# Dense products in pairs on half of the array's rows, with weights in common pieces

## What is computed

```python
def first_block(x, ...):                       # 1 layer
    proj = rmsnorm(x, norm_mix) @ w_in         # q, kv, gates, GLA q k v, merge gates
    o_a = nsa_attention(...)                   # compressed + selected + window softmax
    o_b = gla_chunked(...)                     # gated linear attention
    merged = gate_a * (o_a @ w_up_nsa) + gate_b * (o_b @ w_up_gla)
    x = x + merged @ w_out
    h = rmsnorm(x, norm_ffn)
    x = x + (silu(h @ w_ffn_gate) * (h @ w_ffn_up)) @ w_ffn_down   # D_FF = 2816
    return rmsnorm(x, norm_final)

def second_block(x, ...):                      # 4 layers: mla0, swa, fox, mla1
    y = branch(x)      # h = x @ w_in; 16-head causal (mla, fox) or windowed (swa) softmax; (o * silu(gate)) @ w_out
    x = layernorm(DEEPNORM_ALPHA * x + y)
```

## Time and profile before

| | |
|---|---|
| median of 3 runs | 1986.87 us (1982.08 to 1987.17) |
| profiled execution | 1982.91 us, its span 1980.8 us |
| PE busy | 1854.9 us, 94% of the span, 10060 matmuls |
| PEld / DVE / ACT / POOL busy | 74% / 50% / 36% / 31% |
| mean granted TensorE clock | 0.976 of full |
| chain that ended last | PE 74%, DVE 18%, ACT 5% |

### The profile page before, as it was taken

How to read it: one execution, slowest core, us unless ns; L and a number is a source line. 1 busy time by engine, 2 the same in 40 slices (tenths; PEclk the granted TensorE clock), 3 DMA queues, 4 the chain that set the end, 5 groups by cost and what they waited for, 6 DMA issues and landing times.

```text
span 1980.8 us, 24915 instructions
## 1 busy us (share of the span) xinstructions
PE 1854.9 (94%) x10060; PEld 1469.7 (74%) x10060; DVE 996.3 (50%) x1964; ACT 717.4 (36%) x1533; POOL 621.6 (31%) x296
## 2 busy tenths in 40 slices
PE   6998799999999999999999989889999999999997
PEld 5777666788888888889666777767777777886665
DVE  4457687421410101144777456674655344576675
ACT  4342255323422222234444234442243233254450
POOL 3332111244344353434212223223423223331221
PEclk9998799999999999999999999989999999999998
DMA  4322110244233232334112222112422222321111
GB/s 158 88 75 56 53 33 22 61 120 138 84 98 107 85 106 85 96 88 93 36 43 77 64 86 65 53 54 64 117 64 75 64 64 71 94 50 44 47 56 61
DMA packets 215026, 148.44 MB, mean 75 GB/s; under 512 B 51952, under 2 KB 197120, under 8 KB 214912
## 3 DMA queue, kind: packets, MB, share of 16 engines
q1 hardware_dynamic: 210160, 135.40, 24.4%
q10 hardware_dynamic: 4752, 11.46, 1.7%
HBM read 144.74 MB, written 2.10 MB: 74 GB/s over the span
## 4 chain that ended last, share of the span: by engine, by line
PE 74%; DVE 18%; ACT 5%; issue 1%; DMA 1%; ACTq 0%; POOL 0%; SPq 0%; DVEq 0%
PE PS L386 19%; PE PS L387 19%; PE PS L388 19%; PE PS L474 6%; PE PS L528 5%; DVE P L1470 3%; PE PS L557 2%; ACT P L1024 2%; DVE X L1403 1%; DVE P L1881 1%; PE PS L687 1%; DVE X L1407 1%; DVE ST L1430 1%; DVE X L1421 1%; DVE sm L1867 1%
## 5 line engine op out<-in xcount | busy, mean ns | idle before, releaser
L1964 POOL TENSOR_TENSOR Wl<-Wr,Wh 128x1024 fp32r<-128x1024 f32 (+5 forms) x292 | 621.4, 2139 | 1321.7 <-ACT Wh L958 1321.7
L386 PE MATMUL PS<-XTl,Wh 128*128 128x512 f32 (+1 forms) x1096 | 416.2, 380 | 12.3 <-DVE XTl L1415 6.7
L387 PE MATMUL PS<-XTh,Wl 128*128 128x512 f32 (+1 forms) x1096 | 412.2, 376 | 0.0
L388 PE MATMUL PS<-XTh,Wh 128*128 128x512 f32 (+1 forms) x1096 | 411.6, 376 | 0.0
L958 ACT CAST Wh<-Wr 128x1024 fp32r<-128x1024 f32 (+5 forms) x292 | 267.6, 936 | 202.3 <-PE PS L388 179.6
L386 PEld LDWEIGHTS PS<-XTl,Wh 128*128 128x128 f32 x1096 | 209.5, 191 | 59.7 <-issue 12.8
L388 PEld LDWEIGHTS PS<-XTh,Wh 128*128 128x128 f32 x1096 | 209.4, 191 | 36.9
L387 PEld LDWEIGHTS PS<-XTh,Wl 128*128 128x128 f32 x1096 | 209.4, 191 | 35.3
L386 PE MATMUL PS<-Wl,XTh 128*128 128x512 f32 (+2 forms) x608 | 228.4, 376 | 3.7 <-DVE XTl L1415 3.7
L388 PE MATMUL PS<-Wh,XTh 128*128 128x512 f32 (+2 forms) x608 | 225.0, 370 | 0.0
L387 PE MATMUL PS<-Wh,XTl 128*128 128x512 f32 (+2 forms) x608 | 224.7, 370 | 0.0
(11 more groups left out here) (309 smaller groups left out, 2452.0 us busy)
## 6 DMA issues: line engine op xcount, KB each, us to landing
Wr<-in_w_in SPq DMA_DIRECT2D x38, 512.0 KB, 3.7
Wr<-in_fox_w_in SPq DMA_DIRECT2D x32, 512.0 KB, 3.9
Wr<-in_w_ffn_gate SPq DMA_DIRECT2D x22, 512.0 KB, 3.8
Wr<-in_w_ffn_up SPq DMA_DIRECT2D x22, 512.0 KB, 3.8
Wr<-in_w_ffn_down SPq DMA_DIRECT2D x22, 512.0 KB, 3.5
Wr<-in_swa_w_in SPq DMA_DIRECT2D x20, 512.0 KB, 3.7
Wr<-in_mla_w_in SPq DMA_DIRECT2D x16, 512.0 KB, 4.1
Wr<-in_mla_w_out SPq DMA_DIRECT2D x16, 512.0 KB, 3.5
```

The lines of the kernel that those rows point to most:

```text
L386: pe.matmul(o, l[0], r[1], start=start, stop=False)
L387: pe.matmul(o, l[1], r[0], start=False, stop=False)
L388: return pe.matmul(o, l[0], r[0], start=False, stop=stop)
L1964: raw.tensor_tensor(l[:, 0:m], r[:, 0:m], h[:, 0:m].bitcast(F), sub).then_inc(*weight_lo.next(i))
```

## The change

- `duo` issues two products together: for each of the three parts one matmul on 64 contraction rows for the one product and one on the other 64 rows for the other product, into different banks. `quad` does this for four products in two pairs, first all on one half of the rows, then swapped. A semaphore, `half_done`, holds a product's second half back until its first half is complete.
- `rows_part`, `outproj` and `first_N` go through it. `first_N` pairs tiles 0, 1 and 2 with each other (`THREE`), in six runs of 12 pairs, and does tile 3 in full rows behind its transposes. `outproj` completes both halves of a tile together: with a norm behind it the order is tile 0 first half, tile 1 first half, tile 0 second half, tile 1 second half, then tile 2, tile 3.
- `four_T` replaces `first_T` everywhere and `proj_T` in part: GLA q and k, the merge gate `gb`, `ua`/`ub`, all FFN gate and up products, the first four gates of mla, the first four products of swa and of fox. Its weights come as pieces of 2 feature blocks by 512 columns for the four products together.
- The groups of the FFN are 8, 8, 6. Single gates, queries and keys between attention steps stay `proj_T` in full rows, and `KX` (the compression) too.

```diff
+            def duo(one, two, h):
+                for n, (x, y) in enumerate(((0, 1), (1, 0), (0, 0))):
+                    ins = [pe.matmul(o, l[x][half(u + h)], r[y][half(u + h)], start=start and n == 0, stop=stop and n == 2)
+                           for u, (o, l, r, start, stop) in enumerate((one, two))]
+                return ins
+            def quad(blocks, first, last, flip, ready):
+                marks, ins = {}, {}
+                for g in range(2):
+                    for x in (0, 2):
+                        e.wait_ge(*([marks[x]] if g else ready(x) + ready(x + 1)))
+                        for n, products in enumerate(blocks):
+                            start, stop = first and g == n == 0, last and g == 1 and n == len(blocks) - 1
+                            ins[x], ins[x + 1] = duo(*[(*p, start, stop) for p in products[x:x + 2]], g ^ flip)
+                        if g == 0:
+                            ins[x + 1].then_inc(*half_done.next())
+                            marks[x] = half_done.now()
+                return ins
...
+                for tiles in THREE:          # THREE = ((0, 1), (2, 1), (2, 0), (1, 0), (1, 2), (0, 2))
+                    e.wait_ge(*[marks[t] for t in tiles if t in marks])
...
+                                e.wait_ge(weight_lo.at(i), *free(bs[t]), normed(before[s], t))
...
+                turn_tile(before[s], 3)
+                e.wait_ge(*free(bs[3]), normed(before[s], 3))
+                for i, a, r in blocks:
+                    ins = mm3(PS[bs[3]][:, 0:n], pair(XT, ALL, r, tile(3)), part(i, a, n), r == 0, r == kts - 1)
...
+                if norm:
+                    for i, h in ((0, 0), (1, 0), (0, 1), (1, 1)):
+                        tile_end(i, h)
+                    for i in (2, 3):
+                        tile_end(i, 0)
+                        if turned:
+                            turn_tile(s, i - 2)
+                        tile_end(i, 1)
+                    if turned:
+                        turn_tile(s, 2)
...
+            for g, n in enumerate((8, 8, 6)):
+                for f in range(f0, f0 + n, 2):
+                    cs = slice(128 * f, 128 * f + 256)
+                    four_T([((nm, f + x), XT, (reader, (nm, f + x))) for nm, reader in (("fg", by_act), ("fu", by_dve)) for x in range(2)],
+                           [(wg[:, :, cs], 0), (wu[:, :, cs], 256)], [normed("mix", 3)], None if f else "ffn")
```

More of the change, by code:

```diff
@@ L404, in proj_T, with four_T @@
                 give(b, *readers)
[L406 to L410, removed]
+            def four_T(products, srcs, ready, s=None):
+                bs = [take(p[0]) for p in products]
+                ws = split(srcs, 512)
+                kts = srcs[0][0].shape[1]
+                for h, c in enumerate(HALF_T if s else [ALL]):
                     if h:
@@ L412, in first_T @@
                         turn_tile(before[s], 3)
[L413 to L419, removed]
@@ L420, in first_T @@
-                for (_, b), (_, _, readers) in zip(ws, products):
-                    give(b, *readers)
+                    for n, (i, j, k) in enumerate(ws):
+                        e.wait_ge(weight_lo.at(i), *([normed(before[s], 2 * h + 1)] if s else ready))
+                        ins = quad([[(PS[b][:, c], part(i, a, 512, 128 * x, 128 * x + 128), pair(p[1], ALL, j + a, c))
+                                     for x, (b, p) in enumerate(zip(bs, products))] for a in range(k)],
+                                   j == 0, j + k == kts, n % 2, lambda x: free(bs[x]))
+                        if j + k < kts and c != HALF_T[0]:
+                            ins[3].then_inc(*weight_used.next())
+                            used[i] = weight_used.now()
@@ L423, in first_N @@
+                for x, p in enumerate(products):
+                    ins[x].then_inc(*done(psum_full, *p[0]))
+                    give(bs[x], *p[2:])
+                used[ws[-1][0]] = psum_full.now()
             def first_N(s, key, src, n, reader):
                 bs = [take((*key, t)) for t in range(NT)]
[L426 to L444, removed]
@@ L445, in first_N, with rows_part @@
                 for t in range(NT):
                     give(bs[t], (reader, (*key, t)))
[L448 to L460, removed]
+            def rows_part(key, bs, i, a1, k, kts, n, flip, lhs, ready):
+                e.wait_ge(weight_lo.at(i))
+                ins = quad([[(PS[b][:, 0:n], pair(lhs, ALL, a1 + a, tile(t)), part(i, a, n)) for t, b in enumerate(bs)] for a in range(k)],
+                           a1 == 0, a1 + k == kts, flip, lambda t: free(bs[t]) + ready(t))
+                if a1 + k == kts:
+                    for t in range(NT):
+                        ins[t].then_inc(*done(psum_full, *key, t))
+                    used[i] = psum_full.now()
+                else:
+                    ins[3].then_inc(*weight_used.next())
+                    used[i] = weight_used.now()
@@ L498, in outproj @@
-                    ins.then_inc(*weight_used.next())
+                    for g in range(2):
+                        for i in range(NT):
+                            if g:
+                                e.wait_ge(marks[i])
+                            ins = tile_part(w, a, i, (a + g) % 2, a == g == 0, False)
+                            if g == 0:
+                                ins[1].then_inc(*half_done.next())
+                                marks[i] = half_done.now()
+                    ins[1].then_inc(*weight_used.next())
```

156 lines of the change are left out of this document (94 added, 62 removed).

## The result

The changed kernel takes **2054.12 us** (2052.25 to 2055.67, 4 runs) beside 1986.09 of the kernel before on the same chip (1982.08 to 1987.17, 4 runs): ratio 1.0346, interval [1.0328, 1.0364]. It is slower by 68 us, outside the predicted range. The profiled execution has a span of 2050.2 us, against 1980.8.

A forecast was written before the change was run, and what follows sets the result against it. It took PE's matmul stream as the bound, with stretches where DVE releases PE. From 1982.9 us it took 69 and added 22, 6, 9, 6 and 1: 1958, carried to the median 1962; range 1922 to 2024.

The forecast's parts named there:

- What bounds the kernel: Whole kernel: mostly a matmul stream on PE, weight loads hidden; pairs could win only 0.013 to 0.020 us per matmul.
- Term 1: Dense product streams: a 512-column pair comes every 0.2145 us, as in float32 score rows; saving 69 us with narrower pairs.
- Rival 1: Matmul streams: pairs cost what full matmuls do, 0.227 to 0.234 us, so 2018 us, slower; chance 0.24.
- Term 2: Norms behind outproj: DVE ready 3.6 us later at four layer norms; 22 us, plus 6 at mix and ffn.
- Term 4: Start of outproj: TensorE waits for banks, about 1.1 us three times and 3 us at mix; 6 us.
- lost savings: Pitch savings not redeemed behind late norms: 5.6 us in four tails, 1 us each at swa and fox first products.
- Term 3: First product of the mla stages: waits for tile 2; costs 5.3 us at mla1, about 4 at mla0, sum 9.
- Term 5: Changes between full and half rows: 0.09 us each, net 1 us; half_done taken at nothing.

The follow-up runs named there:

- tile_by_tile: Changed kernel with tiles 0 and 1 finished one after the other in outproj's tail, not interleaved, still as half-row pairs: 2037.77 us.
- before_tail3: Kernel before with outproj's tail of three contraction blocks instead of four where a norm follows: 2005.83 us, ratio 1.0080.
- full_rows: Changed kernel, order kept, with every half-row pair of the dense products put back as full-row matmuls: 2036.16 us, ratio 1.0238.
- old_joints: Changed kernel with outproj, first_N, first products of ffn, swa and fox and the gates' order as before, pairs elsewhere kept: 1992.45 us, ratio 1.0028.
- full_outproj: Changed kernel with only outproj's matmuls on full rows, in the changed order: 2048.58 us.
- micro: Separate kernel, TensorE alone running streams of 192 matmuls, full rows, pairs or one half, several types and widths: reduced type at 512 columns 0.2267 us each.
- micro2: Second kernel of TensorE alone, varying stationary operand, stationary columns and moving columns: 0.2267 us in outproj's form, with pairs or without.

## Why the prediction was wrong

- **What bounds the kernel**: right. The stream is the bound, 0.013 us per matmul is all that pairs could have won, and loads are hidden.
- **Term 1, the step that failed**: "type is where they differ", said of the float32 score rows, from which the pitch of 0.2145 was taken. The pair pitch is 0.227 in the kernel and 0.2267 alone, so the term is 0 us instead of the 69 forecast. Rows of before could not settle it, but they could have weighed it: the leftover was seen in the reduced type on full rows and not in float32 on half rows; two things differed, and I gave the change to rows. Rival 1 named the other reading, and its threshold of 0.221 decided. The Trainium skill, "TensorEngine Tiling (Array Packing)", The Problem, which promises nothing for a contraction of 128 rows, agrees with the runs.
- **Term 2, norms late**: right in mechanism and nearly in size. 3.6 us were forecast; the table has 4.0 to 4.6 per layer norm, and tile_by_tile and before_tail3 show that DVE's first tile sets it. With term 4 it gives, without the lost savings, 14.4 + 3 + 6 = 23.4 us; undoing outproj gave 23.4. That the two agree to the digit is luck: the norms, mix and the FFN gave more and mla1 took 4.8 back.
- **Term 4, banks**: right as far as shown. Each FFN outproj is 1.04 us longer than in full_rows, where 1.1 was said, and 0.66 to 0.68 of it is TensorE standing for a bank; mix is 3.2 longer for the 3 forecast, 1.4 of it in that wait.
- **Term 3, `first_N`**: right mechanism, mis-sized. The forecast was 5.3 and 4 us; undone, 8.4 and 7.1 come back, and 3.4 for the use at the start that I did not count: 21.8 in the medians for 9. TensorE's timeline shows the wait at tile 2, as forecast but 4.67 us instead of 7.4, and what made the rest:

```profile
1757.47 0.65 PE L476 MATMUL PS<-Wl,XTh 64*128 64x336 f32 x2
1757.92 0.48 PE L476 MATMUL PS<-Wh,XTl 64*128 64x336 f32 x2
...
1765.87 0.65 PE L476 MATMUL PS<-Wl,XTh 64*128 64x336 f32 x2 [4.67 <-DVE XTl L1495]
1766.29 0.51 PE L476 MATMUL PS<-Wh,XTl 64*128 64x336 f32 x2
1766.57 0.51 PE L476 MATMUL PS<-Wh,XTh 64*128 64x336 f32 x2
...
1768.76 0.33 PE L476 MATMUL PS<-Wh,XTl 64*128 64x336 f32 x2
1768.91 0.33 PE L476 MATMUL PS<-Wh,XTh 64*128 64x336 f32 x2
1769.30 0.42 PE L476 MATMUL PS<-Wl,XTh 64*128 64x336 f32 x2
...
1777.58 1.10 PE L523 MATMUL PS<-CST,X 128*128 128x128 f32 x8
1780.24 0.42 PE L389 MATMUL PS<-Wl,XTh 128*128 128x336 f32 x1 [1.56 <-DVE XTl L1495]
```

  The first run of 12 pairs and the first 9 pairs of the second come every 0.28 us, not 0.155: the granted clock is at its lower level (below). From 1768.53 on it is 0.155, with 0.39 where a run of 12 ends and the next begins (1768.91 to 1769.30, and twice more). Behind the last pair TensorE has nothing beside the transposes and comes to tile 3 2.66 us after they begin, where 2.7 was said.
- **The first products of swa and fox**: the term that was missing, about 17.5 us for the 2 I gave as lost savings. `four_T` completes `k0` and the forget gate's product `f` only with the other three, and the copies and sums on DVE that the first score needs start then. I looked for what waits in front of the new quads, not for who waits behind their last matmul.
- **Term 5, mode changes and `half_done`**: right in the stream, where pairs lose nothing. But "6 pairs (1.3 us) or more behind" does not hold in `first_N`: there a run of 12 pairs waits for the run just before it, which costs 0.23 us at each of three changes of run, 0.7 us at each use.

Taking 0 for term 1, my own costs would have given 2018 (rival 1). Redone, they add up to 33.4 us and not 35, and the step of 4 us from the profiled execution to the median, which the forecast has and rival 1 lacks, belongs to them: 2020. The other 34 us are, by the medians: first products with the gates 12.7, `first_N` 21.8 less the 9 forecast, the 5.2 left in old_joints, and 3.8 that the three undone parts give back only together, 34.5 in all. That these close to a us is no proof of each: they are differences of medians.

## What to carry to other kernels

In these runs a matmul cost its columns and a small part that goes with its type; splitting the rows of a full contraction won neither. Batching products (pairs, quads, common pieces) costs where a reader waits for one of them: before merging, look at each product's reader at the stage's ends, at how many banks must be free at once, and at every caller of the helper. Where another engine is the bound behind a stream, the moment at which its first input is complete counts, and one number (the tail's length) moves it by 4 us at each norm. And an experiment shows only what its edit really takes out: full_outproj hit its number and left in place the very wait that it was to remove.

## What the runs showed of the hardware that was not expected

**The clock falls after the longer waits.** The windows of fox's first score (columns as in the earlier trace rows), after:

```profile
1480.00:1485.00 5.00, 2.31 (x22) 1.57 (x18) 4.83 (x11) 0.00 (x0) 0.00 (x0) 1.00 0.43 113
1485.00:1490.00 5.00, 2.69 (x16) 1.82 (x16) 2.16 (x6) 0.00 (x0) 0.00 (x0) 0.54 0.00 0
1490.00:1495.00 5.00, 5.00 (x23) 2.81 (x22) 2.27 (x7) 2.29 (x10) 0.00 (x0) 0.78 0.00 0
1495.00:1500.00 5.00, 5.00 (x23) 4.13 (x22) 4.59 (x10) 3.43 (x10) 1.97 (x1) 1.00 0.00 0
```

TensorE stood from 1482.3 to 1487.3 (4.99 us for `MB`), and the clock (third number from the right) is at 0.54 and then 0.78 of full speed before it is back at 1.00. Before, the same wait was 1.5 us and the window of 1435 to 1440 has 1.00. In mla1's first product it is worse; the first of these windows begins with the end of a wait of 4.09 us:

```profile
1755.00:1760.00 5.00, 4.43 (x26) 4.10 (x28) 4.93 (x8) 1.51 (x2) 4.04 (x2) 0.50 0.11 11
1760.00:1765.00 5.00, 1.20 (x10) 0.77 (x6) 4.23 (x12) 1.37 (x4) 0.00 (x0) 0.81 0.55 161
1765.00:1770.00 5.00, 4.07 (x32) 3.83 (x34) 0.72 (x2) 1.97 (x2) 3.40 (x2) 0.66 0.66 211
```

0.50 is the 1.2 GHz level. Before, four windows from 1700 to 1720 all have 1.00. The twelve pairs from 1757.47 take 3.25 us from the first start to the last instead of 1.71 at 0.155, the nine from 1765.87 take 2.66 instead of 1.40: 2.8 us together. Over the span the mean granted clock fell from 0.976 to 0.968, that is from 47.5 to 65.6 us short of full speed; 18 us more are an upper bound of what this cost, since part of it passed while TensorE stood still. It also differs between executions of the same code, as in the swa stage above: 194.7 us at a granted clock of 0.91, 190.9 at 0.94. The Trainium skill, "TensorE: Matmul & The Clock Gate", Why this matters for your kernels, warns of idle gaps of that kind, and the trace agrees. Here a wait of 4 us cost more than 4 us.

**Small matmuls have a floor that rows don't lift.** In `micro`, 128 columns of the reduced type come every 0.1117 us where streaming is 0.0533, PEld busy all the time (20.00 of 20.00), and `micro2` has 0.1117 for 192 columns too, where I had expected 0.0933. The pairs of 128 columns come at the same 0.1117. That the loads are this floor is not shown: at 256 columns PEld is busy all the time as well, and the pitch there is 0.1200. bfloat16 at 512 columns is 0.2158, 5% below the reduced type: that is the 0.011 us per matmul that this change looked for.
